# Expert weights streamed in 4 MB transfers with 32 KB rows through five slots, and expert activations turned by 64x64 products

## The chip, the cores and the metric

The kernel runs on one core of one Trainium2 chip. The metric is the device time of one execution in microseconds (us), as the median of the runs; lower is better. In profiles, PE is TensorE (PEld its weight loads), DVE is VectorE, ACT is ScalarE, POOL is GpSimd, and SP is SyncE, which only issues transfers here. All data is float32.

## What is computed

One layer of a streaming encoder for 256 tokens of width 1024: a time-mixing recurrence, a gated MLP with a spatial mix, and a mixture of experts. The change touches only the last part (and the loading of its constants):

```python
x = x + (g_a * y_a + g_b * y_b) @ w_out
x = x + moe_ffn(rms_norm(x, norm2_g), ...)      # top 4 of 32 experts
# per expert e, for the tokens that chose it:
hgu  = xt[tok] @ w_gate_up[e] + b_gate_up[e]    # 1024 x 2048 weights, 8 MB
gate = jnp.minimum(hgu[:, 0::2], 7.0)
up   = jnp.clip(hgu[:, 1::2], -7.0, 7.0)
act  = gate * jax.nn.sigmoid(1.702 * gate) * (up + 1.0)
y    = act @ w_down[e] + b_down[e]              # 1024 x 1024 weights, 4 MB
```

The weights of all 32 experts are read once: 12 MB an expert, 384 MB (402.7 million bytes) in all.

## The kernel before

The kernel has one instruction stream for each engine; semaphores tie them together. The order inside each stream is written out by hand. A first part of some 350 us computes the two mixers, the output projection and the router. Then comes the expert part, `moe(p)`, whose first pass handles up to 64 tokens (slots) for each expert; further passes run only if an expert has more tokens.

**The weight stream.** SP issues all the expert weights in a fixed list of pieces (`load(n)`, L421). A piece is 2 MB: 16 KB in each of 128 partitions, one contiguous row of memory for each partition. Four pieces hold the gate/up weights of an expert (two k tiles of 128 inputs each), two pieces hold its down weights. The list runs: gate/up of expert 0, then for e = 1 to 31 gate/up of e and down of e-1, and at the end down of 31, whose second half is cut into two pieces of 1 MB. Piece n goes to slot n mod 10 of a ring of ten slots of 16 KB in each partition. These slots lie where the first part of the kernel kept its data, so the first ten loads are gated: five wait for `y_done`, two for `m_ready`, three for `out_done`. From piece 10 on, SP waits for `pieces_read`, which PE raises after its last product with a piece.

**PE's order for expert e** (`moe` in the PE block): `gate_up(p, e, k)` for k = 0 to 7 (L1566), four products of 64 slots by 512 columns each, in pairs that run side by side on the two halves of the array's columns; each product of float32 shows as two MATMUL records. After k = 2 come the biases (L1575), `token_rows(e-1)` (L1596), `turn_acts(e-1)` (L1604) and `scatter(e-2)` (L1613), and, in odd experts, after k = 0 and k = 5 half of the `gather` for the next pair of experts (L1553). After k = 7 comes `down(e-1)` (L1586), 16 products. After the last expert there follow `token_rows(31)`, `turn_acts(31)`, `scatter(30)`, `down(31)` and `scatter(31)`, and then the final norm and the stores.

**The activations.** The gate/up result lies with a slot in each partition: partitions 0 to 63 hold one half of the columns, 64 to 127 the other. DVE (L1111 to L1118) and ACT (L712) turn it into `acts`, PE turns `acts` with four transposes of 128x128 into the bank `DN_BANK`, and ACT copies that to `aT` (L706), the stationary side of `down`. `DN_BANK` also takes the result of `down`, which ACT copies to `ysl` (L701, the last one L692). So `turn_acts` waits for `act_ready` and for `ysl_out`.

Of the kernel before, what the change touches and what calls it, by code (L numbers as in the profile page):

```python
# [6 lines left out]
P = 128  # L7
# [29 lines left out]
for _name, _n in (("ident", P), ("before", P), ("ones", P), ("iota_slot", 2 * SLOTS), ("iota_exp", EXPERTS),  # L37
                  ("gmask", P), ("headones", P), ("causal", P), ("carry", T), ("half_ident", CH), ("centre", CH)):
    CST[_name] = (_at, _n)
    _at += _n  # L40
# [3 lines left out]
def constants():  # L44
# [18 lines left out]
    put("half_ident", p % HD == np.arange(HD)[None, :])  # L63
    put("centre", (p % HD == np.arange(HD)[None, :]) - 1.0 / HD)
# [3 lines left out]
def build(nc, cst, x, norm1_g, w_in, b_gate, time_mix, w_decay_up, w0, a_up, a0, g_up, k_k, k_a, r_k,  # L68
# [8 lines left out]
    with ctx:  # L77
# [68 lines left out]
        n2row = at("n2row", FRONT + 17 * KB, 2 * P, parts=4)  # L146
# [25 lines left out]
        PIECE = 4 * FF  # L172

        HALF = D // 2
        SLOT_AT = [SREG + 16 * KB * i for i in range(4)] + [VREG, QREG + 8 * KB, QREG + 24 * KB, WREG, WREG + 16 * KB, XREG]
        RING = len(SLOT_AT)
        ring = [at(f"ring{i}", off, PIECE) for i, off in enumerate(SLOT_AT)]
# [58 lines left out]
        ring_full = [sem(f"ring_full{i}") for i in range(RING)]  # L236

# [98 lines left out]
        PIECES = EXPERTS * 6 + 1  # L336
        FILLS = [len(range(slot, PIECES, RING)) for slot in range(RING)]

        def gu_piece(e, i):
            return i if e == 0 else 6 * e - 2 + i  # L340

        def dn_pieces(e):

            first = 6 * e + 8 if e < EXPERTS - 1 else PIECES - 3
            if e < EXPERTS - 1:
                return [(first, 0, range(4)), (first + 1, 1, range(4))]
            return [(first, 0, range(4)), (first + 1, 1, range(2)), (first + 2, 1, range(2, 4))]
# [8 lines left out]
        def more_passes(eng, one_pass):  # L356

            with eng.register("more_passes") as count:
# [6 lines left out]
                with eng.If_ne(count, 1):  # L365
                    last = eng.value_load(npass[0:1, 0:1], min_val=1, max_val=T // SLOTS)
                    with eng.Fori(1, last) as p:
                        one_pass(p)

# [13 lines left out]
        def _(sp):  # L383
# [25 lines left out]
            gu_v = w_gate_up[0].rearrange("e (k p two) n -> e k p (two n)", p=P, two=2)  # L409
            dn_v = w_down[0].rearrange("e (j p four) n -> e j p (four n)", p=P, four=4)  # L410

            pieces = [gu_v[0, k, :, :] for k in range(KT // 2)]
            for e in range(1, EXPERTS):
                pieces += [gu_v[e, k, :, :] for k in range(KT // 2)]
                pieces += [dn_v[e - 1, j, :, :] for j in range(2)]
            pieces += [dn_v[EXPERTS - 1, 0, :, :], dn_v[EXPERTS - 1, 1, :, 0:2 * D], dn_v[EXPERTS - 1, 1, :, 2 * D:4 * D]]
            assert len(pieces) == PIECES

            def load(n):
                lo = 2 * D * (n == PIECES - 1)  # L420
# [1285 lines left out]
```

## Time and profile before

| | |
|---|---|
| time, median of 3 runs | 1286.52 us (1286.02 to 1288.03) |
| the profiled execution: its time, its span | 1286.55 us, 1284.7 us |
| PE busy, and its loads | 1207.2 us, 585.9 us |
| DVE, ACT busy | 296.3 us, 169.7 us |
| moved by DMA | 447.83 MB, mean 349 GB/s |
| chain that ended last | PE 54%, DMA 42%, DVE 2% |
| most of its DMA share | gate/up weights into the ring, 38% |

The span is the time from the first to the last instruction of the profiled execution. Matmul records overlap, so the busy time of PE says that it had work, not that it ran at its peak. The chain that ended last is followed back from the last instruction, at each step to what released it. A transfer's time to landing runs from its issue, so it contains the time that it waited behind others.

### The profile page before, as it was taken

How to read it: one execution, taken by the hardware profiler on the slowest of the kernel's cores; microseconds unless marked ns; L12 is line 12 of the kernel's file. 1: busy time of each engine (PE TensorE's matmuls, PEld its weight loads, DVE VectorE, ACT ScalarE, POOL GpSimd, SP SyncE). 2: the span in 40 equal slices, each digit the busy share in tenths (PEclk: the TensorE clock that was granted, in tenths of full speed). 3: DMA queues.
4: the chain of work that ended last, by engine and by line, in shares of the span. 5: the costliest groups of instructions: out<-in, count | busy, mean ns of one | idle time of the engine just before them, and what ended most of it. 6: DMA issues, size and time to landing. Idle time of an engine off the chain costs nothing.

```text
span 1284.7 us, 16843 instructions
## 1 busy us (share of the span) xinstructions
PE 1207.2 (94%) x7521; PEld 585.9 (46%) x7521; DVE 296.3 (23%) x649; ACT 169.7 (13%) x337; POOL 12.7 (1%) x27
## 2 busy tenths in 40 slices
PE   5999999999999999999998989999998989999986
PEld 4788768876533433433233333333332323333322
DVE  1156463334322111121111111111211111111111
ACT  2333212221200000000000000000000000000002
POOL 1000000001000000000000000000000000000000
PEclk9999999999999999999999999999999999999999
DMA  9441568223999999999999999999999999999994
GB/s 239 111 126 45 190 187 206 79 73 136 385 427 428 427 427 428 427 429 427 427 429 427 427 429 426 429 426 430 426 429 426 428 427 427 429 426 428 427 427 194
DMA packets 82975, 447.83 MB, mean 349 GB/s; under 512 B 13866, under 2 KB 52912, under 8 KB 58192
## 3 DMA queue, kind: packets, MB, share of 16 engines
q1 hardware_dynamic: 72672, 440.19, 84.2%
q0 software_dynamic: 1520, 4.36, 1.1%
q10 hardware_dynamic: 8704, 2.12, 0.8%
q8 instruction: 62, 1.02, 0.3%
q14 instruction: 17, 0.14, 0.0%
HBM read 444.56 MB, written 2.10 MB: 348 GB/s over the span
## 4 chain that ended last, share of the span: by engine, by line
PE 54%; DMA 42%; DVE 2%; ACTq 1%; issue 0%; ACT 0%; SPq 0%; DVEq 0%
DMA ring<-w_gate_up 38%; PE ps L1566 19%; PE ps L1159 8%; PE ps L1586 5%; PE ps L1260 4%; DMA ring<-w_down 3%; PE ps L1613 3%; PE ps L1453 2%; PE ps L1247 2%; PE ps L1553 2%; PE ps L1575 2%; ACTq L627 1%; PE ps L1604 1%; PE ps L1196 1%; PE ps L1596 1%; DMA consts<-cst 1%
## 5 line engine op out<-in xcount | busy, mean ns | idle before, releaser
L1566 PE MATMUL ps<-ring,xT 128*64 128x512 f32 x2048 | 463.0, 597 | 34.1 <-DMA ring<-w_gate_up 32.7
L1566 PEld LDWEIGHTS ps<-ring,xT 128*64 128x64 f32 x2048 | 141.3, 136 | 325.2 <-issue 293.3
L1586 PE MATMUL ps<-ring,aT 128*64 128x512 f32 x1024 | 228.2, 594 | 17.9 <-DMA ring<-w_down 17.9
L1586 PEld LDWEIGHTS ps<-ring,aT 128*64 128x64 f32 x1024 | 73.7, 137 | 168.9 <-issue 145.6
L1111 DVE TENSOR_SCALAR gc<-ps 128x512 f32<-128x512 f32 x32 | 22.1, 692 | 407.6 <-PE ps L1566 407.6
L1159 PE MATMUL ps<-hT,wbuf 128*128 128x256 f32 (+1 forms) x432 | 99.8, 386 | 2.8 <-DVE hT L749 2.8
L1066 DVE TENSOR_TENSOR xT<-ps,vec 128x512 f32<-128x512 f32 x32 | 22.1, 692 | 344.4 <-PE ps L1553 344.4
L1159 PEld LDWEIGHTS ps<-hT,wbuf 128*128 128x128 f32 (+1 forms) x432 | 81.0, 190 | 18.1 <-issue 3.1
L1260 PE MATMUL ps<-hT,wbuf 128*128 128x256 f32 x384 | 85.9, 382 | 0.2 <-ACT mb L588 0.2
L1260 PEld LDWEIGHTS ps<-hT,wbuf 128*128 128x128 f32 x384 | 72.1, 190 | 11.9 <-issue 2.3
L1553 PEld LDWEIGHTS ps<-oh,xacc 128*128 128x128 f32 x512 | 62.8, 196 | 25.4 <-issue 24.3
L1553 PE MATMUL ps<-oh,xacc 128*128 128x128 f32 x512 | 68.8, 288 | 0.9 <-DVE oh L1029 0.9
L712 ACT ACTIVATE sgm<-gc 128x512 f32<-128x512 f32 x32 | 20.2, 631 | 368.3 <-DVE gc L1111 368.3
L1613 PE MATMUL ps<-ysl,oht 64*128 64x512 f32 x256 | 63.6, 615 | 0.7 <-ACT ysl L692 0.7
L704 ACT ACTIVATE oht<-ps 128x256 f32<-128x256 f32 x32 | 12.3, 384 | 257.4 <-PE ps L1596 257.4
L701 ACT ACTIVATE ysl<-ps 128x512 f32<-128x512 f32 x31 | 18.5, 597 | 193.6 <-PE ps L1586 193.6
L1575 PE MATMUL ps<-biases,consts 32*64 32x512 f32 x256 | 34.8, 612 | 0.0
L1118 DVE TENSOR_TENSOR gc<-uc,sgm 128x512 f32<-128x512 f32 x32 | 34.1, 1067 | 1.8 <-ACT sgm L712 0.8
L1613 PEld LDWEIGHTS ps<-ysl,oht 64*128 64x128 f32 x256 | 22.0, 186 | 21.8 <-issue 20.3
L1453 PE MATMUL ps<-wbuf,XM 128*128 128x512 f32 x64 | 29.0, 600 | 0.3 <-DVE XM L941 0.3
L1247 PE MATMUL ps<-wbuf,hT 128*128 128x512 f32 x64 | 28.0, 592 | 0.0
L1114 DVE SCALAR_TENSOR_TENSOR uc<-uc,gc 128x512 f32<-128x512 f32 x32 | 22.1, 692 | 1.1
(257 smaller groups left out, 662.2 us busy)
## 6 DMA issues: line engine op xcount, KB each, us to landing
ring<-w_gate_up SPq DMA_DIRECT2D x128, 2048.0 KB, 42.4
ring<-w_down SPq DMA_DIRECT2D x63, 2048.0 KB, 41.4
wbuf<-w_in SPq DMA_DIRECT2D x26, 512.0 KB, 4.1
wbuf<-w_in SPq DMA_DIRECT2D x12, 1024.0 KB, 6.6
wbuf<-w_in SPq DMA_DIRECT2D x2, 2048.0 KB, 10.1
wbuf<-w_out SPq DMA_DIRECT2D x8, 512.0 KB, 4.1
ring<-w_down SPq DMA_DIRECT2D x2, 1024.0 KB, 41.1
xacc<-x SPq DMA_DIRECT2D x2, 512.0 KB, 4.1
```

Of the source, the lines that this page charges most:

```text
L1066: V.tensor_tensor(by_k(xT[pair % 2][:, :])[:, 4 * half:4 * half + 4, :], by_k(bank(b)), vec[:, r:r + 4].unsqueeze(2).to_broadcast([P, 4, 2 ...
L1111: V.tensor_scalar(gc[:, :], pairs[:, 0, :], LIMIT, None, ALU.min).then_inc(sm["gc_ready"], 1)
L1118: V.tensor_tensor(acts[:, :].rearrange("q (r p) -> q p r", r=4), by_row(uc), by_row(sgm), MUL).then_inc(sm["act_ready"], 1)
L1159: last = mm(proj_slot(n)[0:w, :], wv[:, k, 0:w], hv[:, k, :], start=k == 0, stop=k == KT - 1)
L1247: last = mm(bank(m_), hv[:, k, tb * P:(tb + 1) * P], wv[:, k, :], start=k == 0, stop=k == KT - 1)
L1260: last = mm(f_slot(t), wv[:, k, P * (t % 2):P * (t % 2) + P], hv[:, k, :], start=k == 0, stop=k == KT - 1, skip_group_check=True)
L1453: last = mm(bank(2 * tb + half_), XM_v[:, k, tb * P:(tb + 1) * P], unit((k + 4) % 8)[:, 512 * half_:512 * half_ + 512], start=k == 0, stop ...
L1553: last = mm(bank(b, (k % 4) * 2 * SLOTS, 2 * SLOTS), xacc[:, lo:lo + 2 * P - 1:2], oh[pair % 2][:, tb * 2 * SLOTS:(tb + 1) * 2 * SLOTS], s ...
L1566: last = mm(bank(GU_BANK + q, 0, 512, slice(64 * half, 64 * half + 64)), x_, w[:, r0 + D * half + 512 * q:r0 + D * half + 512 * (q + 1)], ...
L1575: mm(bank(GU_BANK + q, 0, 512, slice(64 * half, 64 * half + 64)), ident[r, 32 * q + e:32 * q + e + 1].to_broadcast([32, SLOTS]), bgu[r, HA ...
L1586: last = mm(bank(DN_BANK, 0, 512, slice(64 * half, 64 * half + 64)), aT[:, c0:c0 + SLOTS], w[:, D * r + 512 * half:D * r + 512 * (half + 1 ...
L1613: last = mm(bank(OUT_BANK + 2 * tb + half), oht[e % 2][r, tb * P:(tb + 1) * P], ysl[r, :], start=e == 0 and isinstance(p, int), stop=False ...
```

## The change

- A piece is 4 MB: 32 KB in each of 128 partitions, one contiguous row for each. Gate/up of an expert is two pieces (four k tiles each), down is one. There are 96 pieces, five slots of 32 KB; the ring holds as many bytes as before. The last piece is loaded by four transfers of 1 MB with a semaphore for each (`part_full`).
- The gated first loads are two, one and two pieces.
- A partition of a gate/up piece now holds four neighbouring rows of the weights instead of two, so `gather` picks every fourth column of the tokens instead of every second, and the second copy of the norm's weights is laid out the same way (four small transposes at the start instead of two).
- A partition of the down piece holds eight neighbouring rows. So the activations have to be turned in chunks of 64 columns: `turn_acts` is 16 products of 64x64 with a new constant `half_turn`, instead of four transposes of 128x128. DVE writes `acts` with a stride of 8 instead of 4.
- The waits for `act_ready` and `ysl_out` are moved from `turn_acts` to the head of `token_rows`, which stands ahead of it.

```diff
 CST, _at = {}, 0
-for _name, _n in (("ident", P), ("before", P), ("ones", P), ("iota_slot", 2 * SLOTS), ("iota_exp", EXPERTS),
+for _name, _n in (("ident", P), ("before", P), ("ones", P), ("iota_slot", 2 * SLOTS), ("iota_exp", EXPERTS), ("half_turn", SLOTS),
                   ("gmask", P), ("headones", P), ("causal", P), ("carry", T), ("half_ident", CH), ("centre", CH)):
...
     put("iota_exp", np.arange(EXPERTS)[None, :])
     put("half_ident", p % HD == np.arange(HD)[None, :])
...
-        n2row = at("n2row", FRONT + 17 * KB, 2 * P, parts=4)
+        n2row = at("n2row", FRONT + 17 * KB, 4 * P, parts=2)
 
         vsb = at("vsb", FRONT, TB * D)
         mb = at("mb", FRONT + 8 * KB, KT * T)
@@ -169,11 +170,12 @@
         sgb = [at(f"sgb{b}", FRONT + 63 * KB + KB * b, T) for b in range(2)]
         sga = [at(f"sga{b}", FRONT + 65 * KB + KB * b, T) for b in range(2)]
         t1 = at("t1", FRONT + 67 * KB, KT * HD)
-        PIECE = 4 * FF
+        PIECE = 8 * FF
 
         HALF = D // 2
-        SLOT_AT = [SREG + 16 * KB * i for i in range(4)] + [VREG, QREG + 8 * KB, QREG + 24 * KB, WREG, WREG + 16 * KB, XREG]
+        SLOT_AT = [SREG, SREG + 32 * KB, QREG + 8 * KB, WREG, VREG]
         RING = len(SLOT_AT)
+        LAST_PARTS = 4
         ring = [at(f"ring{i}", off, PIECE) for i, off in enumerate(SLOT_AT)]
         m4 = Map(CST["gmask"][0] * 4, CST_W * 4)
         gt = m4.take("gt", T)
@@ -234,6 +236,7 @@
                  "y_out yk_done yn_ready ysl_out ysq_out z_copied zeroed ").split()
         sm = {n: sem(n) for n in names}
         ring_full = [sem(f"ring_full{i}") for i in range(RING)]
+        part_full = [sem(f"part_full{i}") for i in range(LAST_PARTS - 1)]
 
         class Own:
 
@@ -333,18 +336,14 @@
 
 
 
-        PIECES = EXPERTS * 6 + 1
+        PIECES = EXPERTS * 3
         FILLS = [len(range(slot, PIECES, RING)) for slot in range(RING)]
         def gu_piece(e, i):
-            return i if e == 0 else 6 * e - 2 + i
-
-        def dn_pieces(e):
-
-            first = 6 * e + 8 if e < EXPERTS - 1 else PIECES - 3
-            if e < EXPERTS - 1:
-                return [(first, 0, range(4)), (first + 1, 1, range(4))]
-            return [(first, 0, range(4)), (first + 1, 1, range(2)), (first + 2, 1, range(2, 4))]
+            return i if e == 0 else 3 * e - 1 + i
+
+        def dn_piece(e):
+            return 3 * e + 4 if e < EXPERTS - 1 else PIECES - 1
...
-            gu_v = w_gate_up[0].rearrange("e (k p two) n -> e k p (two n)", p=P, two=2)
-            dn_v = w_down[0].rearrange("e (j p four) n -> e j p (four n)", p=P, four=4)
-
-            pieces = [gu_v[0, k, :, :] for k in range(KT // 2)]
+            gu_v = w_gate_up[0].rearrange("e (k p four) n -> e k p (four n)", p=P, four=4)
+            dn_v = w_down[0].rearrange("e (p eight) n -> e p (eight n)", p=P, eight=8)
+
+            pieces = [gu_v[0, 0], gu_v[0, 1]]
             for e in range(1, EXPERTS):
-                pieces += [gu_v[e, k, :, :] for k in range(KT // 2)]
-                pieces += [dn_v[e - 1, j, :, :] for j in range(2)]
-            pieces += [dn_v[EXPERTS - 1, 0, :, :], dn_v[EXPERTS - 1, 1, :, 0:2 * D], dn_v[EXPERTS - 1, 1, :, 2 * D:4 * D]]
+                pieces += [gu_v[e, 0], gu_v[e, 1], dn_v[e - 1]]
+            pieces += [dn_v[EXPERTS - 1]]
             assert len(pieces) == PIECES
 
             def load(n):
-                lo = 2 * D * (n == PIECES - 1)
-                sp.dma_start(ring[slot_of(n)][:, lo:lo + pieces[n].shape[-1]], pieces[n]).then_inc(ring_full[slot_of(n)], 16)
+                parts = LAST_PARTS if n == PIECES - 1 else 1
+                w = PIECE // parts
+                for i in range(parts):
+                    sp.dma_start(ring[slot_of(n)][:, i * w:(i + 1) * w], pieces[n][:, i * w:(i + 1) * w]).then_inc(part_full[i - 1] if i else ring_full[slot_of(n)], 16)
 
             sp.wait_ge(sm["y_done"], NCH)
-            for n in range(5):
-                load(n)
+            load(0)
+            load(1)
             sp.wait_ge(sm["m_ready"], KT * NCH)
-            load(5)
-            load(6)
+            load(2)
             sp.wait_ge(sm["out_done"], 2 * TB)
-            for n in range(7, RING):
-                load(n)
+            load(3)
+            load(4)
...
-                    n = gu_piece(e, 3)
+                    n = gu_piece(e, 1)
...
-                    by_row = lambda t: t[:, :].rearrange("q (p r) -> q p r", r=4)
-                    V.tensor_tensor(acts[:, :].rearrange("q (r p) -> q p r", r=4), by_row(uc), by_row(sgm), MUL).then_inc(sm["act_ready"], 1)
+                    by_row = lambda t: t[:, :].rearrange("q (p r) -> q p r", r=8)
+                    V.tensor_tensor(acts[:, :].rearrange("q (r p) -> q p r", r=8), by_row(uc), by_row(sgm), MUL).then_inc(sm["act_ready"], 1)
...
-            tr(bank(4, P, 4), n2row[:, 0:2 * P - 1:2], ident[0:4, 0:4])
-            tr(bank(4, P + 4, 4), n2row[:, 1:2 * P:2], ident[0:4, 0:4]).then_inc(sm["vec_ps"], 1)
+            for r in range(4):
+                last = tr(bank(4, P + 2 * r, 2), n2row[:, r:r + 4 * P - 3:4], ident[0:2, 0:2])
+            last.then_inc(sm["vec_ps"], 1)
...
             def gather(pair, k, b, tbs):
 
                 for tb in tbs:
-                    lo = tb * D + 2 * P * (k // 2) + k % 2
-                    last = mm(bank(b, (k % 4) * 2 * SLOTS, 2 * SLOTS), xacc[:, lo:lo + 2 * P - 1:2], oh[pair % 2][:, tb * 2 * SLOTS:(tb + 1) * 2 * SLOTS],
+                    lo = tb * D + 4 * P * (k // 4) + k % 4
+                    last = mm(bank(b, (k % 4) * 2 * SLOTS, 2 * SLOTS), xacc[:, lo:lo + 4 * P - 3:4], oh[pair % 2][:, tb * 2 * SLOTS:(tb + 1) * 2 * SLOTS],
                               start=tb == 0 and k % 4 == 0, stop=tb == TB - 1, skip_group_check=True)
...
             def gate_up(p, e, k):
-                n, r0 = gu_piece(e, k // 2), 2 * D * (k % 2)
+                n, r0 = gu_piece(e, k // 4), 2 * D * (k % 4)
                 w = ring[slot_of(n)]
-                if k % 2 == 0:
+                if k % 4 == 0:
                     pe.wait_ge(ring_full[slot_of(n)], 16 * fill_of(p, n))
                 x_ = xT[e // 2 % 2][:, (2 * k + e % 2) * SLOTS:(2 * k + e % 2 + 1) * SLOTS]
                 for q in range(2):
                     for half in range(2):
                         last = mm(bank(GU_BANK + q, 0, 512, slice(64 * half, 64 * half + 64)), x_, w[:, r0 + D * half + 512 * q:r0 + D * half + 512 * (q + 1)],
                                   start=k == 0, stop=k == KT - 1, skip_group_check=True)
-                if k % 2:
+                if k % 4 == 3:
                     last.then_inc(sm["pieces_read"], 1)
...
             def down(p, e):
                 pe.wait_ge(sm["at_out"], after(p, e + 1))
-                for n, j, rs in dn_pieces(e):
-                    w = ring[slot_of(n)]
-                    pe.wait_ge(ring_full[slot_of(n)], 16 * fill_of(p, n))
-                    for r in rs:
-                        c0 = r * P + j * SLOTS
-                        for half in range(2):
-                            last = mm(bank(DN_BANK, 0, 512, slice(64 * half, 64 * half + 64)), aT[:, c0:c0 + SLOTS],
-                                      w[:, D * r + 512 * half:D * r + 512 * (half + 1)], start=j == 0 and r == 0, stop=j == 1 and r == 3)
-                    last.then_inc(sm["pieces_read"], 1)
+                n = dn_piece(e)
+                w = ring[slot_of(n)]
+                pe.wait_ge(ring_full[slot_of(n)], 16 * fill_of(p, n))
+                for r in range(8):
+                    if e == EXPERTS - 1 and r and r % 2 == 0:
+                        pe.wait_ge(part_full[r // 2 - 1], 16 * after_pass(p))
+                    for half in range(2):
+                        last = mm(bank(DN_BANK, 0, 512, slice(64 * half, 64 * half + 64)), aT[:, r * SLOTS:(r + 1) * SLOTS],
+                                  w[:, D * r + 512 * half:D * r + 512 * (half + 1)], start=r == 0, stop=r == 7)
+                last.then_inc(sm["pieces_read"], 1)
 
             def token_rows(p, e):
 
+                pe.wait_ge(sm["act_ready"], after(p, e + 1))
+                if e:
+                    pe.wait_ge(sm["ysl_out"], after(p, e))
                 pe.wait_ge(sm["og_ready"], after(p, e + 1))
                 if e:
                     pe.wait_ge(sm["oht_out"], after(p, e))
@@ -1597,11 +1604,10 @@
                 last.then_inc(sm["oht_done"], 1)
 
             def turn_acts(p, e):
-                pe.wait_ge(sm["act_ready"], after(p, e + 1))
-                if e:
-                    pe.wait_ge(sm["ysl_out"], after(p, e))
-                for j in range(4):
-                    last = tr(bank(DN_BANK, j * P, P), acts[:, j * P:(j + 1) * P], ident)
+                for r in range(8):
+                    for half in range(2):
+                        rows = slice(64 * half, 64 * half + 64)
+                        last = mm(bank(DN_BANK, r * SLOTS, SLOTS, rows), acts[rows, r * 64:(r + 1) * 64], C("half_turn", rows), start=True, stop=True)
                 last.then_inc(sm["at_done"], 1)
```

SP's queue at the start of the weight stream, before: the rows from the first weight load on (126 to 135 are the ten slots, 4096 the floats in each partition).

```order
L421 DMA ring_126<-w_gate_up 128x4096 [waits y_done]
L421 DMA ring_127<-w_gate_up 128x4096
L421 DMA ring_128<-w_gate_up 128x4096
L421 DMA ring_129<-w_gate_up 128x4096
L421 DMA ring_130<-w_gate_up 128x4096
L421 DMA ring_131<-w_gate_up 128x4096 [waits m_ready]
L421 DMA ring_132<-w_gate_up 128x4096
L421 DMA ring_133<-w_gate_up 128x4096 [waits out_done]
L421 DMA ring_134<-w_down 128x4096
L421 DMA ring_135<-w_down 128x4096
L421 DMA ring_126<-w_gate_up 128x4096 [waits pieces_read]
L421 DMA ring_127<-w_gate_up 128x4096 [waits pieces_read]
```

After:

```order
L424 DMA ring_126<-w_gate_up 128x8192 [waits y_done]
L424 DMA ring_127<-w_gate_up 128x8192
L424 DMA ring_128<-w_gate_up 128x8192 [waits m_ready]
L424 DMA ring_129<-w_gate_up 128x8192 [waits out_done]
L424 DMA ring_130<-w_down 128x8192
L424 DMA ring_126<-w_gate_up 128x8192 [waits pieces_read]
L424 DMA ring_127<-w_gate_up 128x8192 [waits pieces_read]
L424 DMA ring_128<-w_down 128x8192 [waits pieces_read]
```

The same gates stand ahead of 10, 4 and 6 MB before and of 8, 4 and 8 MB after, and a load waits for the reading of a whole 4 MB slot.

PE's stream at its end, before: `down(30)` from two pieces, `token_rows(31)`, `turn_acts(31)`, `scatter(30)`, and the start of `down(31)` (one row here is a product, not a MATMUL record).

```order
L1586 MATMUL ps<-ring_134,aT 64x512 [waits ring_full8,at_out]
L1586 MATMUL ps<-ring_134,aT 64x512 x7
L1586 MATMUL ps<-ring_135,aT 64x512 [waits ring_full9]
L1586 MATMUL ps<-ring_135,aT 64x512 x7
L1596 MATMUL ps<-consts,og_160 128x128 [waits oht_out,og_ready]
L1596 MATMUL ps<-consts,og_160 128x128
L1604 MATMUL ps<-consts,gc 128x128 [waits ysl_out,act_ready]
L1604 MATMUL ps<-consts,gc 128x128 x3
L1613 MATMUL ps<-ysl,oht_163 128x512 [waits oht_out,ysl_out]
L1613 MATMUL ps<-ysl,oht_163 128x512 x3
L1582 ISA [waits at_out]
L1586 MATMUL ps<-ring_126,aT 64x512 [waits ring_full0]
```

After, the same stretch:

```order
L1590 MATMUL ps<-ring_130,aT 64x512 [waits ring_full4,at_out]
L1590 MATMUL ps<-ring_130,aT 64x512 x15
L1603 MATMUL ps<-consts,og_155 128x128 [waits og_ready,oht_out,ysl_out,act_ready]
L1603 MATMUL ps<-consts,og_155 128x128
L1610 MATMUL ps<-consts,gc 64x64 x16
L1619 MATMUL ps<-ysl,oht_158 128x512 [waits oht_out,ysl_out]
L1619 MATMUL ps<-ysl,oht_158 128x512 x3
L1585 ISA [waits at_out]
L1590 MATMUL ps<-ring_126,aT 64x512 [waits ring_full0]
L1590 MATMUL ps<-ring_126,aT 64x512 x3
L1588 ISA
L1590 MATMUL ps<-ring_126,aT 64x512 [waits part_full0]
```

All 16 products of `down(30)` now stand behind one wait for the landing of 4 MB, `token_rows` waits for `ysl_out`, the four transposes have become 16 products, and `down(31)` waits part by part.

## Rows read from the trace of the kernel before

**Rows 1.** Page, the span in 40 slices of 32.1 us: GB/s moved.

```profile
GB/s 239 111 126 45 190 187 206 79 73 136 385 427 428 427 427 428 427 429 427 427 429 427 427 429 426 429 426 430 426 429 426 428 427 427 429 426 428 427 427 194
```

**Rows 2.** Windows: length, busy by engine (count), TensorE clock, DMA share, GB/s.

```profile
340.00:520.00 180.00, 177.59 (x910) 71.61 (x910) 37.04 (x92) 17.49 (x31) 0.55 (x1) 1.00 1.01 427
520.00:1200.00 680.00, 637.68 (x3132) 240.90 (x3130) 108.27 (x210) 51.83 (x94) 0.00 (x0) 1.00 1.01 428
```

**Rows 3.** Chain that ended last, steady part: start, length, what.

```profile
633.76 44.28 DMA ring<-w_gate_up
...
692.53 44.23 DMA ring<-w_gate_up
```

**Rows 4.** Waits: who for whom, us in total, times, longest.

```profile
PE ps L1566 <- DMA ring<-w_gate_up: 32.7, 33, 2.0
```

**Rows 5.** Chain that ended last, while PE was behind the transfers.

```profile
413.27 6.87 PE ps L1586 x32
...
442.23 6.87 PE ps L1586 x32
...
466.72 6.87 PE ps L1586 x32
```

**Rows 6.** Page, DMA issues: line, count, KB each, us to landing.

```profile
ring<-w_gate_up SPq DMA_DIRECT2D x128, 2048.0 KB, 42.4
ring<-w_down SPq DMA_DIRECT2D x63, 2048.0 KB, 41.4
...
ring<-w_down SPq DMA_DIRECT2D x2, 1024.0 KB, 41.1
```

**Rows 7.** Page, DMA queues: packets, MB, share of 16 engines' span.

```profile
q10 hardware_dynamic: 8704, 2.12, 0.8%
q8 instruction: 62, 1.02, 0.3%
```

**Rows 8.** Tile ring: last issue of 2 MB, last issue of 1 MB, landings.

```profile
L421 SPq DMA_DIRECT2D ring<-w_down x1: 328/328/328, 1222.1 to 1222.1; - x1
...
DMA to landing us min/median/max: 42.7/42.7/42.7
...
L421 SPq DMA_DIRECT2D ring<-w_down x1: 328/328/328, 1229.4 to 1229.4; - x1
...
DMA to landing us min/median/max: 40.4/40.4/40.4
```

**Rows 9.** Chain that ended last, the tail.

```profile
1218.69 41.29 DMA ring<-w_down
...
1260.02 3.68 PE ps L1586 x16
...
1263.72 0.61 ACT ysl L701
...
1264.47 0.63 PE ps L1604 x4
1265.10 1.92 PE ps L1613 x8
1267.01 7.04 PE ps L1586 x32
```

**Rows 10.** Chain again, earlier: `token_rows` with nothing to wait for.

```profile
428.54 0.37 PE ps L1596 x2
```

**Rows 11.** Timeline of PE: products of 64x64 in the first part.

```profile
296.44 1.15 PE L1382 MATMUL ps<-ub,BK 64*64 64x64 f32 x32
```

**Rows 12.** Tile ring: the two `m_ready` issues and their landings.

```profile
L421 SPq DMA_DIRECT2D ring<-w_gate_up x2: 328/381/434, 325.8 to 326.1; - x2
...
DMA to landing us min/median/max: 26.3/29.2/32.0
```

**Rows 13.** Timeline of SP: the first issue behind `out_done`.

```profile
342.48 0.33 SPq L421 DMA_DIRECT2D ring<-w_gate_up  x1
```

**Rows 14.** Groups of PE's weight loads: the gather, tokens at stride 2.

```profile
L1553 PEld LDWEIGHTS ps<-oh,xacc 128*128 128x128 f32 x512 | 62.8, 196 | 25.4 <-issue 24.3 <-DVE oh L1029 1.0
```

More of the change, by code:

```diff
@@ L63, in constants @@
     put("half_ident", p % HD == np.arange(HD)[None, :])
+    put("half_turn", p % HD == np.arange(HD)[None, :])
     put("centre", (p % HD == np.arange(HD)[None, :]) - 1.0 / HD)
@@ L368, in more_passes, with after_pass @@
                         one_pass(p)
+        def after_pass(p):
+            return p + 1
         def after(p, e):
@@ L460, in _ @@
             rows("norm2", norm2_g[0])
-            pool.dma_start(n2row[:, :], norm2_g[0].rearrange("(r p) -> r p", p=2 * P)).then_inc(misc[1], 16)
+            pool.dma_start(n2row[:, :], norm2_g[0].rearrange("(r p) -> r p", p=4 * P)).then_inc(misc[1], 16)
             rows("mix_k", time_mix[0, D:2 * D])
@@ L698, in moe @@
                     if e >= 2:
-                        n = dn_pieces(e - 2)[-1][0]
+                        n = dn_piece(e - 2)
                         act.wait_ge(sm["pieces_read"], p * PIECES + n + 1)
@@ L744, in _ @@
             V.tensor_copy(vec[:, 0:VROWS], bank(4, 0, VROWS)).then_inc(sm["vec_ready"], 1)
-            V.tensor_copy(vec[:, VROWS:VROWS + KT].rearrange("p (i r) -> p r i", r=2), bank(4, P, KT).rearrange("p (r i) -> p r i", r=2)).then_inc(sm["vec_ready"], 1)
+            V.tensor_copy(vec[:, VROWS:VROWS + KT].rearrange("p (i r) -> p r i", r=4), bank(4, P, KT).rearrange("p (r i) -> p r i", r=4)).then_inc(sm["vec_ready"], 1)
             dve.wait_ge(sm["vec_ready"], 2)
```

## The prediction

> **What bounds the kernel now.** I read the slices first, then windows, waits, the chain and the landings.
>
> The slices show when the weight stream begins: the rate jumps to 385 GB/s in the eleventh slice and then stays at 426 to 430 in every slice up to the last but one [rows 1]. The windows say the same of two stretches: 427 GB/s from 340 to 520 us and 428 from 520 to 1200, with the DMA engines' share at 1.01 in both [rows 2]. So the transfers never stop for want of a free slot, and 402.7 million bytes at 428 GB/s are 941 us of the span. PE is not the bound: in the steady part the chain enters the transfers at 633.76 and again at 692.53 [rows 3], 58.77 us for two experts, which is 12 transfers of 2 MB, 4.90 us each. What PE needs for two experts is read where it was behind and waited for nothing: from 413.27 to 466.72, 53.45 us, of which the odd expert, which also gathers, takes 28.96 and the even one 24.49 [rows 5]. PE thus has 5.3 us to spare in each pair and spends it waiting for landings: 33 waits of at most 2.0 us for gate/up weights [rows 4]. Before about 520 us PE lags behind the stream, later it waits for it.
>
> The end hangs on one landing. The first half of down(30)'s weights is not on the path, the second half lands at 1218.69 + 41.29 = 1259.98 [rows 9]. Then come 8 products (3.68 us), ACT's copy to `ysl`, the transposes, `scatter(30)` and the 16 products of `down(31)`, whose own weights land, by issue plus time to landing, from 1222.1 + 42.7 = 1264.8 (2 MB) to 1229.4 + 40.4 = 1269.8 (the last MB) [rows 8], before PE needs them. So the time is: when the stream's last but one 4 MB have landed, plus a serial tail. Both ends of that sum are changed.
>
> **Part 1, larger rows and transfers.** One record of a transfer is one row of one partition. Before there are 191 transfers of 128 rows of 16 KB and 2 of 128 rows of 8 KB [rows 6]: 24,704 rows, 1544 on each of 16 engines. After there are 95 x 128 rows of 32 KB and 4 x 128 of 8 KB: 12,672, or 792 on each. That is 752 fixed costs fewer on each engine; what is one worth? The trace has no row of 32 KB. From above: the 8704 packets of q10 average 244 bytes and take 0.8% of 16 engines' span, 0.008 x 1284.7 x 16 / 8704 = 18.9 ns each [rows 7]; a 16 KB row takes 4.90 us / 8 = 612 ns [rows 3]. A line through the two has a fixed part of 9.9 ns, so at most 752 x 10 ns = 7.5 us are saved. From below: the last two transfers of 1 MB with rows of 8 KB land 5.0 us after the 2 MB before them, where one transfer of 2 MB with 16 KB rows takes 4.90 [rows 3, 8]: 8 more rows on each engine cost 0.1 us with 0.1 us of rounding in the landings, anything from 0 to 25 ns a row. The lower end is therefore 0. I take 5 ns, the middle, since the long rows of the stream are the nearer case and the short packets of q10 probably carry waits that a long row hides: **-3.8 us** (ends 0 and -7.5).
>
> The Trainium skill (DMA: Bandwidth & Descriptors, "Why small descriptors are slow (HBM only)") gives a fixed overhead of some 3 cycles a packet inside the DMA engine; at the 850 MHz of its section "Where 436 GB/s comes from" that is 3.5 ns, an estimate of 2.7 us saved, and the sum below would be 1288.6.
>
> **Part 2, the ring.** It stays as deep in bytes, but the gates let 12 instead of 14 MB through before `out_done`. The two transfers of the `m_ready` gate land at 325.8 + 26.3 = 352.1 and 326.1 + 32.0 = 358.1 [rows 12]; SP passes `out_done` at 342.48 [rows 13]. With one transfer fewer in the queue the stream would still run to 352.1, 9.6 us past that. The next load waits for all four k tiles of expert 0's first piece instead of two; PE reads them by 359 us (its first product begins at 351, and four k tiles with the biases take 8 us, by the rates of [rows 5]), while what is queued by then lasts to about 373 (20 MB, two transfers and a third past 358.1). Later PE frees a slot at most 12 us after its landing, with three whole slots, 29 us, queued. **0 us**; if that cover were gone, each us without a queued load would cost one.
>
> **Part 3, the tail.** `down(30)` is behind one landing of 4 MB, at the same place of the stream. All its 16 products run after it: 6.87 [rows 5] instead of 3.68 us [rows 9], **+3.2**. `token_rows(31)` used to run while ACT copied `ysl` (1263.72 to 1264.33), now it waits for that copy and adds its own 0.37 us [rows 10], **+0.4**. The 16 products of 64x64 are 32 records; 32 such records take 1.15 us [rows 11], against 0.63 for the transposes [rows 9], **+0.5**. ACT's copy to `aT` hides under `scatter(30)` (1.92 us) as before. `down(31)` begins 11.4 us after the landing, its last MB has landed 9.8 us after it (1269.8), so it doesn't wait for parts. One thing must hold: that PE stands waiting when down(30) lands. From the landing of expert 31's first half, 19.5 us earlier, PE has an even-like load (31 gathers nothing): 24.49 less `down` 6.87 plus 0.5 is 18.1 us. It holds by 1.4 us. Sum of the tail **+4.1**.
>
> **Part 4, small things.** PE's products of 64x64 add 28 matmuls and 28 weight loads an expert, 1792 instructions to the 16,843 of the page; their code comes by DMA: 62 packets of 16 KB, 1.02 MB [rows 7]. At the same bytes per instruction that is 7 packets more, some 0.6 us each, on engines that are full. Spread evenly they cost 0.3 us, on one engine 4; I take **+0.5**. The constants grow from 656 to 688 KB and two small transposes more stand at the start, on the path: **+0.2**. In the middle, `turn_acts` costs PE 0.5 us an expert and DVE's stride more on a path that isn't bound: the pair needs 54.5 us against 58.5 from the stream, so PE catches up later than 520 us (16 us of lag at 4.0 a pair: some 590), long before the end. 0 us.
>
> **Sum:** -3.8 + 4.1 + 0.5 + 0.2 = +1.0 us, made against the profiled execution (1286.55, its span 1284.7). That is 0.03 us from the median, so the forecast is **1287.5**. About 0.2%, 2.6 us, is what a measurement of this kernel tells from no change, so this is "the same".
>
> **The rivals.**
>
> *The stream gains nothing (slower).* If the row's cost goes by bytes alone, or the hardware cuts rows at 16 KB, only the tail is left: +4.1 + 0.7 = 1291.3. For it: the near-equal landings of 8 KB and 16 KB rows [rows 8]. Against it: q10's packets, which do show a fixed part. It counts as slower from a cost below 2.9 ns a row. Chance 0.27.
>
> *The stream gains all of it (faster).* At 10 ns a row the saving is 7.5 us: 1286.5 - 7.5 + 4.8 = 1283.8. Decided from 9.8 ns a row on, that is by a steady pair of experts (47 rows fewer on each engine) at 58.3 us or less rather than 58.5. For it: the line through q10's packets, and that a fixed cost for each transfer (99 instead of 193) would come on top. Chance 0.17.
>
> *Rows 32 KB apart slow the memory side (slower).* All 16 engines then read at places twice as far apart; each percent of rate lost is 9.4 us, so 1% gives 1287.5 + 3.8 + 9.4 = 1300.7. No row here bears on it: all ring transfers have one spacing. The Trainium skill (DMA: Bandwidth & Descriptors, "Latency and other measured facts") reports such losses for row pitches of 512 KB and more at powers of two, with gaps between the rows read; ours stay contiguous and 32 KB apart, so I leave it a chance of 0.05.
>
> *PE becomes the bound (slower).* The gather's loads take 196 ns at stride 2 [rows 14]. If stride 4 made each of the 32 of a pair longer by 4.0 / 32 = 0.12 us or more, PE would need more than the stream gives; at twice that it is 4.0 us over in each of 16 pairs, up to 60 us. Nothing speaks for so steep a cost. Chance 0.03.
>
> **How the numbers follow.** Within 0.2%: costs from 2.9 to 9.8 ns a row, chance 0.48. Slower: 0.27 + 0.05 + 0.03 = 0.35. Faster: 0.17. The range for 8 in 10 goes from 1283, the full saving, to 1292, the tail with no saving and a few packets of code on one engine; what is beyond it are the memory side, PE as the bound, and gains above any row's. The forecast's own range is 1284 to 1289.
>
> **What the profile after would show.** Part 1: ring rates of 429 to 431 GB/s in windows from 520 to 1200, and a pair of experts at 58.4 to 58.6 us; 428 and 58.8 for the first rival. Part 2: a rate of 425 or more already from 345 us, and no window of the stream below it. Part 3: one wait of PE's first product of `down(30)`, then 6.9 us of it, `token_rows` behind the copy of `ysl`, 32 records of 64x64 in about 1.1 us, and some 28.8 us from the landing to the end where it was 24.7. Part 4: about 69 instruction packets. The forecast would be wrong if the rate moved by more than a percent either way, if PE were late at the landing of down(30), or if the stream showed a gap near 342 us.

## The result

The changed kernel takes **1304.8 us** (median of 4 runs, 1303.6 to 1306.5) against 1286.7 us (median of 4, 1286.0 to 1288.0): ratio 1.014, 95% interval 1.012 to 1.016. It is 18 us slower; the forecast was no change. The profiled execution took 1306.5 us with a span of 1304.7, 20.0 us above the span of before.

Its page, the slices of the span (32.6 us each): PE, DMA busy in tenths, then the rate. And the groups of the gather and of the turned activations (busy us, mean ns of one).

```profile
PE   6999999999999999999999999999999999999997
...
DMA  9441668224999999999999999989999999999990
GB/s 236 114 129 36 194 181 211 66 99 165 395 431 432 427 429 429 433 431 431 426 430 431 433 427 428 378 370 429 410 432 430 430 430 431 431 429 432 430 388 35
...
L1556 PEld LDWEIGHTS ps<-oh,xacc 128*128 128x128 f32 x512 | 121.9, 328 | 25.4 <-issue 24.3
...
L1610 PE MATMUL ps<-consts,gc 64*64 64x64 f32 x1024 | 36.7, 221 | 0.0
```

The rate in most slices of the expert part is higher than before [rows 1], but the last slice moves almost nothing, and in no slice between the first and the last is PE less than 90% busy. The gather's loads have gone from 196 [rows 14] to 328 ns. The chain that ended last is all PE:

```profile
PE 98%; DVE 1%; issue 0%; ACT 0%; DVEq 0%
```

and its steady part reads (start, length, what), two experts from one `down` to the next but one:

```profile
1051.28 6.87 PE ps L1590 x32
1058.14 5.15 PE ps L1569 x24
1063.29 1.02 PE ps L1578 x8
1064.31 0.37 PE ps L1603 x2
1064.68 1.08 PE ps L1610 x32
1065.76 1.92 PE ps L1619 x8
1067.67 8.73 PE ps L1569 x40
1076.41 6.87 PE ps L1590 x32
...
1084.99 3.93 PE ps L1556 x16
...
1109.70 6.87 PE ps L1590 x32
```

Not one wait for a landing. A pair of experts takes 58.42 us (1051.28 to 1109.70) where PE alone needed 53.45 before [rows 5]: half a gather is 3.93 us instead of 2.08, twice a pair, and the turn is 1.08 instead of 0.44, twice a pair. The old times, from the chain before:

```profile
421.86 2.08 PE ps L1553 x16
...
428.91 0.44 PE ps L1604 x4
```

The transfers wait for PE: a gate/up transfer lands 19.0 us after its issue, where it was 42.4 [rows 6] and where the same 4 MB transfers take 36.0 once the gather is repaired (first experiment), because the queue ahead of it is short. The stream's last transfer is issued at 1253.0 us and, with at most 19.0 us to landing, is in some 16 us before PE begins its last `down` at 1287.8.

**Where 20.0 us come from.** The gather: 512 records, 32 blocks of 16, 1.85 us more each, 59.2 us. The turns: 32 x 0.64 = 20.5 us. Both are on PE's chain from the first expert on. At 837 us, in expert 16 (where PE has 7.8 us of other work to do, before and after), the granted TensorE clock falls to 0.50, its lower level (1.2 GHz), for about 7 us, while PE works without a pause; three groups there take 4.39, 3.61 and 7.70 us where before they took 3.63, 1.87 and 6.87: 3.3 us. Before, then after:

```profile
813.89 3.63 PE ps L1535 x8
817.52 1.87 PE ps L1566 x8
819.38 6.87 PE ps L1586 x32
```

```profile
833.86 4.39 PE ps L1538 x8
838.25 3.61 PE ps L1569 x8
841.86 7.70 PE ps L1590 x32
```

The new order at the tail adds 0.7. Together 84 us more on PE's chain, of which 64 went into time that it used to spend waiting for landings (84 less the 20.0 that show).

### The profile page after: what moved, and what is told of

It reads as the page before. It is cut to its first block, busy times and chain, and to the rows that moved or that the text cites. A ratio compares the mean times of both kernels' runs of the same rounds, so it can differ in the third digit from the quotient of the medians.

```text
span 1304.7 us, 18544 instructions
## 1 busy us (share of the span) xinstructions
PE 1278.6 (98%) x8419; PEld 664.3 (51%) x8419; DVE 296.5 (23%) x649; ACT 169.7 (13%) x337; POOL 12.7 (1%) x27
## 4 chain that ended last, share of the span: by engine, by line
PE 98%; DVE 1%; issue 0%; ACT 0%; DVEq 0%
PE ps L1569 35%; PE ps L1590 17%; PE ps L1556 10%; PE ps L1162 7%; PE ps L1263 6%; PE ps L1619 5%; PE ps L1610 3%; PE ps L1578 2%; PE ps L1456 2%; PE ps L1250 2%; PE ps L1603 1%; PE ps L1199 1%; PE ps L1219 0%; PE ps L1301 0%; PE ps L1172 0%; PE ps L1179 0%
## 5 line engine op out<-in xcount | busy, mean ns | idle before, releaser
L1556 PEld LDWEIGHTS ps<-oh,xacc 128*128 128x128 f32 x512 | 121.9, 328 | 25.4 <-issue 24.3
L1556 PE MATMUL ps<-oh,xacc 128*128 128x128 f32 x512 | 128.1, 405 | 0.9 <-DVE oh L1031 0.9
L1610 PE MATMUL ps<-consts,gc 64*64 64x64 f32 x1024 | 36.7, 221 | 0.0
L1610 PEld LDWEIGHTS ps<-consts,gc 64*64 64x64 f32 x1024 | 32.3, 134 | 5.3 <-issue 5.3
L1120 DVE TENSOR_TENSOR gc<-uc,sgm 128x512 f32<-128x512 f32 x32 | 34.1, 1067 | 1.8 <-ACT sgm L714 0.8
```

Source lines behind the costliest of these rows:

```text
L1120: V.tensor_tensor(acts[:, :].rearrange("q (r p) -> q p r", r=8), by_row(uc), by_row(sgm), MUL).then_inc(sm["act_ready"], 1)
L1556: last = mm(bank(b, (k % 4) * 2 * SLOTS, 2 * SLOTS), xacc[:, lo:lo + 4 * P - 3:4], oh[pair % 2][:, tb * 2 * SLOTS:(tb + 1) * 2 * SLOTS], s ...
L1610: last = mm(bank(DN_BANK, r * SLOTS, SLOTS, rows), acts[rows, r * 64:(r + 1) * 64], C("half_turn", rows), start=True, stop=True)
```

## The experiments

**Three theories.** A: PE became the bound, through the gather's strided loads and the turns together. B: the stream of 32 KB rows through five slots is what costs. C: the clock's dip. The first four kernels take PE's extra work out of the changed kernel, or put it into the kernel before. They leave out the right order of the features or rows; the sizes and counts of the products stay as in the kernel that each follows, except where a turn is exchanged.

**The changed kernel with stride 2 in the gather**

```diff
-                    lo = tb * D + 4 * P * (k // 4) + k % 4
-                    last = mm(..., xacc[:, lo:lo + 4 * P - 3:4], ...)
+                    lo = tb * D + 2 * P * (k // 2) + k % 2
+                    last = mm(..., xacc[:, lo:lo + 2 * P - 1:2], ...)
```

> The kernel after the change with the gather's token columns read at stride 2 again (the wrong tokens' features are gathered, the count and shape of all instructions stay). Theory A, PE became the bound through the gather's weight loads at stride 4 and the 64x64 turns, and it never catches up with the stream: 512 records at 0.115 us less each take 58.9 us from PE's chain, the stream bounds again, and the time is 1284 to 1288 us. Theory B, the stream of 32 KB rows through five slots is what costs (a lower rate, or slots that free too late): the time stays above 1300. Theory C, the TensorE clock's dips make the difference: 1300 to 1303, wherever PE still binds.

Measured 1285.0 us (ratio 0.999, 0.998 to 1.000). With every transfer, slot and 64x64 product of the change in place, the loss is gone (19.8 us less than the changed kernel). Theory B falls. So does C as the main cause: the mean granted clock was 0.991 here and 0.993 in the changed kernel. The chain has landings again:

```profile
1139.60 35.16 DMA ring<-w_gate_up
...
1197.89 35.69 DMA ring<-w_gate_up
```

The two entries stand 58.29 us apart, against 58.77 [rows 3]. Single distances vary (57.39 and 58.65 earlier in the same chain), so the better measure of the stream's own pace is the rate from 520 to 1200 us, 431 GB/s against 428 [rows 2]: some 58.4 us a pair with rows of 32 KB, 58.8 before.

**The kernel before with stride 4, and with stride 4 and the 64x64 turns.** The first has the edit above the other way round. The second also has the change's `turn_acts`, its waits in `token_rows` and its constant; its transfers stay at 2 MB and its slots at ten.

> The kernel before with the gather's token columns at stride 4 and nothing else changed (features in the wrong order). Theory A: PE's chain alone would end some 20 us earlier than after the change (the turns' 32 x 0.64 us are missing), at a span of about 1280, just short of the stream's 1284.7: time 1286 to 1290 us. Rival A2, the gather's loads alone explain the whole loss: 1300 or more. Theory B: 1286.6.

Measured 1286.8 us (ratio 1.000, 0.999 to 1.001). Its loads take 328 ns, and one landing of expert weights is left on its chain, that of `down(30)`:

```profile
1226.34 35.13 DMA ring<-w_down
...
1261.51 3.68 PE ps L1586 x16
```

> The kernel before, with its 2 MB transfers and ten slots, and only PE's extra work of the change: gather at stride 4, activations turned by 16 products of 64x64, the two waits at the head of the token rows (features in the wrong order). Theory A: PE's chain is that of the changed kernel, 1300 to 1307 us. Theory B: 1286 to 1288, since the stream is untouched. A count by pace alone (PE 58.4 us a pair of experts, under the stream's 58.8) would also give 1287 to 1289.

Measured 1306.8 us (ratio 1.015, 1.013 to 1.018), with no landing of expert weights on the chain and a mean granted clock of 0.997. So the whole loss appears with the old stream. And the stride alone, worth 59 us of PE's time, costs nothing: PE still has just enough of the old waits to give. This also refutes a count by pace: PE's 58.4 us a pair are less than the old stream's 58.8, and yet the kernel is 20 us slower. In the changed kernel PE and stream both need 58.4 us, and no count by pace gives 20 us there either. DVE's strided write of `acts` is no part of it: it takes 1067 ns with a stride of 8 as with 4.

**The changed kernel with transposes of 128x128**

```diff
-                for r in range(8):
-                    for half in range(2):
-                        rows = slice(64 * half, 64 * half + 64)
-                        last = mm(bank(DN_BANK, r * SLOTS, SLOTS, rows), acts[rows, r * 64:(r + 1) * 64], C("half_turn", rows), ...)
+                for j in range(4):
+                    last = tr(bank(DN_BANK, j * P, P), acts[:, j * P:(j + 1) * P], ident)
```

> The kernel after the change with the activations turned by four transposes of 128x128 again (rows in the wrong order for the down weights); stride 4 and the 4 MB transfers stay. Theory A: PE's chain is 20.5 us shorter, ends at a span of about 1280 to 1284, near the stream's own end: 1282 to 1287 us. Theory B: above 1300. Theory C: above 1300 if the clock dips stay.

Measured 1285.6 us (ratio 0.999, 0.998 to 1.000). Taking out the smaller part gives as much as taking out the larger: either alone fits into PE's spare time, both do not. PE's loads in this kernel still take 328 ns, it waits for no ring transfer, and it begins `down(30)` at 1257.32, some 2 us after the weights land when the stream is the bound (1254.98, in the kernel with the turned copy below). So here PE and the stream end almost together.

**What a stride costs.** One kernel, one column set for each stride.

```diff
-                    last = mm(..., xacc[:, lo:lo + 2 * P - 1:2], ...)
+                    if k == 0:
+                        last = mm(o_, xacc[:, 0:128:1], i_, **f_)
+                    if k == 1:
+                        last = mm(o_, xacc[:, 0:255:2], i_, **f_)
...
+                    if k == 7:
+                        last = mm(o_, xacc[:, 0:2033:16], i_, **f_)
```

> The kernel before with each of the gather's eight column sets read at a stride of its own: 1, 2, 3, 4, 6, 8, 12 and 16 floats (wrong features), each on its own line. Theory P, a load's time goes with the bytes that it spans beyond what the array takes: 196 ns up to stride 2, 328 at 4, some 650 at 8 and 1300 at 16. Theory K, there is one step between dense and strided reads: the same 328 ns or so from stride 3 or 4 on, whatever the stride. The whole time tells little, since the sets differ.

The groups of its weight loads; strides 1, 2, 3, 4, 6, 8, 12, 16 stand on the lines 1555, 1557, 1559, 1561, 1563, 1565, 1567, 1569.

```profile
L1567 PEld LDWEIGHTS ps<-oh,xacc 128*128 128x128 f32 x64 | 18.7, 368 | 0.0
...
L1565 PEld LDWEIGHTS ps<-oh,xacc 128*128 128x128 f32 x64 | 16.8, 334 | 0.0
...
L1561 PEld LDWEIGHTS ps<-oh,xacc 128*128 128x128 f32 x64 | 16.4, 327 | 0.0
L1569 PEld LDWEIGHTS ps<-oh,xacc 128*128 128x128 f32 x64 | 15.8, 315 | 0.0
L1563 PEld LDWEIGHTS ps<-oh,xacc 128*128 128x128 f32 x64 | 15.5, 312 | 12.2 <-issue 12.2
...
L1559 PEld LDWEIGHTS ps<-oh,xacc 128*128 128x128 f32 x64 | 12.6, 262 | 0.0
...
L1557 PEld LDWEIGHTS ps<-oh,xacc 128*128 128x128 f32 x64 | 8.9, 197 | 0.0
L1555 PEld LDWEIGHTS ps<-oh,xacc 128*128 128x128 f32 x64 | 8.4, 190 | 13.2 <-issue 12.2 <-DVE oh L1029 1.0
```

Stride 2 costs 7 ns more than stride 1, from 2 to 4 each step costs 65 ns, and from 4 to 16 it stays between 312 and 368. Theory K holds with a ramp instead of a step; theory P falls. Each row is a mean over 64 loads of one execution, so the order among the strides from 4 on should not be leaned on.

**The change without its stride: a turned copy.** DVE's residual sum writes the tokens once in the order that the gather wants, into a buffer of its own; the gathered tokens' buffers take the old one's place.

```diff
-                V.tensor_tensor(o, o, bank(2 * tb + half), ADD).then_inc(sm["o_out"], 1)
+                turned = lambda a: a.rearrange("q (p r) -> q r p", r=4)
+                xo = xp[:, tb * D + HALF * half:tb * D + HALF * (half + 1)].rearrange("q (r p) -> q r p", r=4)
+                V.tensor_tensor(xo, turned(o), turned(bank(2 * tb + half)), ADD).then_inc(sm["o_out"], 1)
...
-                           w_router[0].rearrange("(k p) n -> p k n", p=P)).then_inc(sm["late_in"], 16)
+                           w_router[0].rearrange("(h p r) n -> p h (r n)", h=2, r=4)).then_inc(sm["late_in"], 16)
...
-                    last = mm(..., xacc[:, lo:lo + 4 * P - 3:4], ...)
+                    last = mm(..., xp[:, tb * D + k * P:tb * D + (k + 1) * P], ...)
```

> The kernel after the change, computing the same result, with the stride taken out of the gather: the residual sum of the tokens is written by DVE once in turned order (four column sets of 128 in a row for each half), the router's weights are loaded in that order, and the gather reads 128 neighbouring columns. Theory A (PE's gather loads were the bound): like the run with stride 2, the stream at some 58.3 us a pair bounds, 1284 to 1287 us. Rival: DVE's strided sum on the path to the router, or a moved buffer, costs it back: 1288 or more.

Measured 1285.2 us (ratio 0.999, 0.998 to 1.000), loads at 195 ns. This is the change as it was priced in the forecast, so its tail answers to the tail before [rows 9]:

```profile
1217.37 37.62 DMA ring<-w_down
1254.98 0.14 issue
1255.12 7.09 PE ps L1593 x32
1262.20 0.73 issue
1262.94 0.41 PE ps L1606 x2
1263.35 1.08 PE ps L1613 x32
1264.43 1.92 PE ps L1622 x8
1266.35 7.04 PE ps L1593 x32
```

The last landing on the chain comes at 1254.98 instead of 1259.98, 5.0 us earlier, and from there to the end of the span (1283.4) it is 28.4 us instead of 24.7. PE had stood idle for 1.36 us when it came.

**What a row costs.** Three kernels load the same pieces in other cuts: two transfers of 2 MB with rows of 16 KB, one transfer of 4 MB with two rows of 16 KB in each partition, four transfers of 1 MB with rows of 8 KB. The first lines below are those of the first and third, the last two those of the second.

```diff
-                    sp.dma_start(ring[slot_of(n)][:, i * w:(i + 1) * w], pieces[n][:, i * w:(i + 1) * w]).then_inc(...)
+                    cut = 1 if i else 2        # or 4
+                    for j in range(cut):
+                        lo, hi = i * w + j * w // cut, i * w + (j + 1) * w // cut
+                        sp.dma_start(ring[slot_of(n)][:, lo:hi], pieces[n][:, lo:hi]).then_inc(...)
...
-            gu_v = w_gate_up[0].rearrange("e (k p four) n -> e k p (four n)", p=P, four=4)
+            gu_v = w_gate_up[0].rearrange("e (k c p two) n -> e k p c (two n)", c=2, p=P, two=2)
```

> The kernel with the turned copy, each 4 MB piece loaded by two transfers of 2 MB with rows of 16 KB (other halves of the same 32 KB). If a row or a transfer has a fixed cost on its DMA engine of 10 ns a row, as the steady pairs of 58.29 against 58.77 us say, the stream is 7.5 us longer: 7 to 8 us above the run with whole pieces. With 5 ns a row it would be 3 to 4 us, with no cost nothing.

Measured 1292.4 us (ratio 1.004, 1.003 to 1.006): 7.2 us above whole pieces. (The first megabyte of the last piece is cut in two as well, 128 rows that don't change the sum.)

> The kernel with the turned copy, each piece one transfer of 4 MB made of two rows of 16 KB in each partition, taken 2 MB apart in memory (the order of the weights' rows then doesn't fit the gather and the turned activations). Theory R, the cost belongs to the row: the same as with two transfers of 2 MB, 7 to 8 us above whole pieces. Theory T, it belongs to the transfer: the same as whole pieces.

Measured 1291.5 us (ratio 1.004, 1.002 to 1.005). That is 6.3 us above whole pieces, so the cost goes with the row. The medians of the two kernels differ by 0.85 us for 96 transfers, which is inside the runs' spread.

> The kernel with the turned copy and each piece loaded by four transfers of 1 MB with rows of 8 KB. With 10 ns a row the stream is 3 x 7.5 = 22.5 us longer than with whole rows and a steady pair takes 58.3 + 1.4 = 59.7 us: 1306 to 1309 us. With a cost that goes by bytes above some length it would be like rows of 16 KB, 1292.

Measured 1305.0 us in one run, 19.8 us above whole pieces, or 18.4 when each is set against the kernel before in its own series (1288.5 in one run, 1287.1). The rates from 520 to 1200 us (the last column) of rows of 32, 16 and 8 KB, in this order, each from its own kernel:

```profile
520.00:1200.00 680.00, 657.43 (x3792) 256.76 (x3790) 107.16 (x208) 51.36 (x94) 0.00 (x0) 0.99 1.00 431
```

```profile
520.00:1200.00 680.00, 650.18 (x3751) 255.08 (x3747) 105.55 (x205) 51.16 (x93) 0.00 (x0) 0.99 1.01 427
```

```profile
520.00:1200.00 680.00, 639.84 (x3664) 251.38 (x3662) 105.51 (x205) 50.18 (x91) 0.00 (x0) 0.99 1.01 421
```

7.2 us for 760 rows more on each engine (95 x 128 / 16) is 9.5 ns a row, 6.3 us is 8.3; 19.8 us for 2280 is 8.7, 18.4 is 8.1. With rows of 8 KB the number of transfers grows too, and SP's issues, 2.1 us and more each, stand on the chain for 23% of the span; the engines' share is 1.01 all the same.

**The tail in parts.** The last three whole pieces come in two transfers each, with a semaphore for each half.

```diff
-                parts = LAST_PARTS if n == PIECES - 1 else 1
+                parts = LAST_PARTS if n == PIECES - 1 else 2 if n >= PIECES - 4 else 1
...
+                    if e == EXPERTS - 2 and r == 4:
+                        pe.wait_ge(half_full[2], 16 * after_pass(p))
```

> The kernel with the turned copy and the last three whole pieces (gate/up of expert 31, down of expert 30) loaded in two transfers of 2 MB each, PE waiting for each half by itself; same result. By the tail's terms down(30) has only 8 products behind its last landing: 3.2 us less than whole pieces, 1281 to 1284 us. Rival: PE comes late to that landing, and it gives 0 to 1.5 us.

Measured **1282.0 us** (ratio 0.996, 0.995 to 0.998), the fastest of all. Its tail has half of `down(30)` behind the landing:

```profile
1254.34 0.04 issue
1254.39 3.65 PE ps L1599 x16
1258.04 0.74 issue
1258.78 0.41 PE ps L1612 x2
```

## Why the prediction was wrong

**The step that failed** is the sentence in part 4 that the pair needs 54.5 us in the middle, "0 us". It took the gather at its old time. The stride went from 2 to 4 and the row of the loads was read [rows 14], but the sum put the cost of stride 4 at nothing, though no row showed a load at that stride, and the case was left at a chance of 0.03 with "Nothing speaks for so steep a cost". The changed kernel and the sweep show it: 328 ns instead of 196, 59 us of PE's time in all, where the old kernel stood at the last stride that costs almost nothing. The turn was too small as well: 0.5 us an expert is its price in the tail (1.15 less 0.63), but in the middle four transposes take 0.44 us, so it is 0.64 and 20.5 us in all. With the stride alone or the turn alone the forecast of no cost in the middle would have stood; both together it did not.

**The rule for when PE binds was wrong too.** The rival named the right mechanism, PE as the bound through the gather's loads, but asked whether PE's pace exceeds the stream's, and put the limit at 0.12 us a record. Measured: 1.85 / 16 = 0.116 us, below that limit, and it did decide. What counts is the sum over the whole expert part. PE starts behind the stream (before, its first expert product at 351 us, the weights' first transfer issued at 313; after, the product at 355) and has 7.8 us of other work in expert 16; equal paces mean that it never makes this up. What it had to give is the sum of its waits for landings: an estimate of 59 us from the trace before (5.3 us in each of the 12.6 pairs from 520 to 1260, less the work in expert 16), 64 by the changed kernel. The turns took 20 of it, so the gather's limit was 39 to 44 us in 512 records, 0.08 to 0.09 us each. The runs show the sum: 59 us fit (1286.8 and, with 4 MB pieces, 1285.6), 20 with 4 MB pieces fit (1285.0), 80 don't (1306.8 and 1304.8).

**Part 1** had the right mechanism and half the size. It took 5 ns a row between 0 and 10; the runs with rows of 32, 16 and 8 KB give 8.1 to 9.5, so the saving is 6 to 7 us instead of 3.8. The line through the short packets of q10 [rows 7], 9.9 ns, was nearly right as it stood; the reason for halving it (they "probably carry waits") was not borne out. The 3 cycles a packet of the Trainium skill (DMA: Bandwidth & Descriptors, "Why small descriptors are slow (HBM only)"), an estimate of 3.5 ns, are less than half of what these runs show.

**Part 2** holds in the main. The rate is 418 GB/s from 340 to 360 us and 434 from 360 to 380, without a gap at 342. From 345 to 360 it is 420, less than the 425 that the forecast asked for; in the kernel with the turned copy it is 427. Five slots never starved the stream where it was the bound.

**Part 3** holds. With the gather repaired the tail is 28.4 us from the landing, forecast 28.8. `down(30)` takes 7.09 us, the copy of `ysl` and `token_rows` 1.14 in a row, the turn 1.08; to the start of `down(31)` that is 11.37 us instead of 7.03, 4.3 more where 4.1 were forecast, and what follows was 0.6 us shorter, which no term of the forecast explains. PE's wait of 1.36 us for the landing matches the margin of 1.4; the margin is thin, for with stride 2 PE goes into `down(30)` without a wait, at 1253.90. In the changed kernel itself the landing no longer mattered.

**Part 4**: 69 instruction packets, as forecast; what they cost can't be told from these runs. Two more small transposes and larger constants at the start were priced at 0.2 us; the four transposes take 0.59 us on the chain where two took 0.34.

**The sum** without the stride, from the measured terms, is -6.1 to -7.2 for the rows and +3.7 for the tail (28.4 less 24.7), -2.4 to -3.5 us; the kernel with the turned copy is 1.9 us below its own reference (1285.2 to 1287.1). In its profiled execution the first expert weights were issued at 314.1 us instead of 313.0, which is 1.1 us of the difference; the small transposes at the start are 0.25 of that, and the changed kernel issued them at 313.3. The rest stays open. The third rival, a memory side that is slower at 32 KB spacing, is refuted by the rate of 431 GB/s.

## What to carry over

- When work is moved between two nearly balanced engines, compare sums over the stretch, not paces. The one that waits can absorb about the total of its waits in the old trace, from which what it is behind at the start is already taken; two additions that are each free can cost their excess together.
- A longer row of a transfer is a new order of the data, and somebody pays for that order. Follow it to each reader and look at its innermost stride; if that grows, write the data once in the new order where an engine has time (here DVE, 1.07 instead of 0.69 us, four times).
- Before a transfer is made larger, count what waits for the last of them. Large pieces in the middle and small ones at the end gave 1282.0 us, where large ones throughout gave 1285.2.

## What the runs showed of the hardware

- TensorE's weight loads of 128x128 float32 take 190 ns at a stride of 1 float, 197 at 2, 262 at 3, 327 at 4 and 312 to 368 from 6 to 16.
- A contiguous row of the weight stream costs its DMA engine 8 to 9.5 ns beside its bytes, about the same from 32 to 16 KB as from 32 to 8 KB; 96 transfers more or less made 0.85 us, inside the spread, when they were queued.
- In the changed kernel the granted TensorE clock fell to 0.50 for some 7 us at 837 us, behind a stretch in which PE hadn't paused, and for some 3 us at 352, just behind a pause (PE busy 0.10 us from 350 to 351). Windows at the first (length, busy by engine, clock, DMA share, GB/s):

```profile
836.00:837.00 1.00, 1.00 (x3) 0.39 (x2) 0.00 (x0) 0.00 (x0) 0.00 (x0) 0.80 1.14 492
837.00:838.00 1.00, 1.00 (x2) 0.00 (x0) 0.00 (x0) 0.00 (x0) 0.00 (x0) 0.50 0.84 360
...
841.00:842.00 1.00, 1.00 (x6) 0.27 (x4) 0.09 (x1) 0.00 (x0) 0.00 (x0) 0.50 0.00 0
```

In the last of these windows nothing is moved: SP waits for a slot until 841.9. From 350 to 360 us the mean clock was 0.74 to 0.83 in the five kernels whose gather reads at strides of 4 or more, in part or throughout, and 1.00 in all the others. What triggers a dip was not tried. Kernels in which the stream is the bound have dips too (mean clock 0.991 with stride 2) and show no loss by them: 1285.0 us there.
